# Self attention's rows are divided by their sums after the values are weighed, squares move to GpSimd, and two pieces of weighing stand one step later

## The chip, the cores and the metric

The kernel runs on one core of one Trainium2 chip. The metric is device time in microseconds (us). TensorE, written PE in the profile, multiplies matrices; ScalarE (ACT) applies functions; VectorE (DVE) and GpSimd (POOL) do elementwise work; SyncE (SP) starts transfers. Each engine runs its own instructions in program order and waits for the others by semaphores.

## The reference, cut to what matters

The program is a whole block with memory attention and feed forward, then two more layers. What is changed is its first mixer, at 512 positions, in float32:

```
fox:   s = q k^T / 8 + c_t - c_s, causal;  p = softmax(s);  o = p v        (8 heads of 64)
chunk: s = q k^T / 8 + bias, chunk-causal; p = softmax(s);  o = p v        (8 heads of 64)
mix = concat(rms_norm(o_fox), rms_norm(o_chunk)) @ w_out
```

`softmax` subtracts the row's maximum, takes `exp` and divides by the row's sum. `rms_norm` needs the sum of the squares of all heads' outputs. The memory, 256 positions of 1024, is normalised in the same stretch of time.

## The kernel before, in words

Every float32 operand of a product is held as a high part in a rounded type and a low part, the remainder; a product is three matmuls, high by high, high by low and low by high (`three`, L942 to L944). The high part is a copy by ScalarE, the low part a subtraction by VectorE or GpSimd.

Self attention is a pipeline of 64 steps. A unit is two heads and eight steps: step s has head 2(s//8) + s%2 and query block (s%8)//2, with 128, 256, 384 or 512 keys. I call a step by j = s%8 and its unit. Units 0 to 3 are the fox heads, 4 to 7 the chunk heads. In one step:

- TensorE `score_pair` makes scores for two heads at once in every second step, four steps ahead.
- VectorE takes the row's maximum (`maximum`, L2667).
- ScalarE takes the exponential, three steps ahead, and the row's sum with it (`exp`, L1915).
- VectorE inverts the sum (`invert`, L2673), and GpSimd multiplies the probabilities by it (`scale`, L854).
- TensorE turns the probabilities, a transpose per tile of 128 keys (`turn`, L1176). It waits for `scale`, and for the low part of two steps before, because there are two banks T.
- ScalarE writes the high part of the turned tile (`pt_high`, L1929), VectorE the low part (`pt_low`, L2680), into PT for even heads and PTH and PTL for odd ones.
- TensorE weighs the values of the unit before (`weigh`), in four pieces a head, a piece for each block of 128 keys, with 512, 384, 256 and 128 queries. The table `WEIGHED_AT` says in which j each piece comes. The values' two parts (VS) stand for both heads side by side, so a head's product fills 128 rows of bank O, of which 64 are its own.
- ScalarE copies those 64 rows into Y (`out`, L1941), even head in step 6, odd head in step 7, and then makes the next unit's high values (`stage_v`, L1908); GpSimd makes the low values (`low_v`, L847).

`pt_high` of step 0 and of step 1 overwrites what pieces (0, 0) and (1, 0) of the unit before read, and waits for them. In these two steps `exp` goes ahead of `pt_high`, and `maximum` ahead of `pt_low`.

Beside this, ScalarE squares the memory in steps 28 to 35 and Y in steps 36 to 63, VectorE adds up the squares (`norm_add`, L2612), scales the memory and makes its low parts in steps 41 to 59 (`self_norms`). After self attention GpSimd makes the low parts of the weight panels of the next product, mem_k (L806, then L902), and TensorE multiplies eight chunks of it; the sums of squares come after chunks 0 and 1 (L1150).

Of the kernel before, what the change touches and what calls it, by code (L numbers as in the profile page):

```python
# [17 lines left out]
F32 = mybir.dt.float32  # L18
F32R = mybir.dt.float32r
# [25 lines left out]
WEIGHED_AT = [[(0, 0), (0, 1)], [(1, 0), (1, 1)], [], [(0, 2)], [(1, 2)], [(0, 3)], [(1, 3)], []]  # L45
# [202 lines left out]
def program(nc, xT, memT, panels, ada, c, vecs, cons, gates_w, bias, pos, outT):  # L248
    ctx = ExitStack()
    with ctx:  # L250
# [88 lines left out]
        SELC = place(152, "SELC", [104, HEADS * P], F32R)  # L339

# [255 lines left out]
        for name in ("self", "mem", "mla"):  # L596
            att[name] = {k: sem(f"{name}_{k}") for k in (
                "v_high", "v_split", "scores", "max", "exp", "recip", "probs", "turned",
                "pt_high", "pt_split", "pv") + (("out",) if name == "self" else ())}
# [29 lines left out]
        def unit_v(name, u):  # L629

            if name == "self":
                return staged_v(V[:, :, u // 4 * S + u % 4 * P:u // 4 * S + u % 4 * P + P], u % 2, P)
# [170 lines left out]
        def _(pool):  # L803
# [53 lines left out]
            def attention(name):  # L857
# [4 lines left out]
                for s in range(steps):  # L862
# [4 lines left out]
                    if name == "self":  # L867
                        if s >= 12 and s % 8 == 7 and s // 8 + 1 < 8:
                            low_v(name, s // 8 + 1)
                        continue  # L870
                    n = (s - 6) // 4
                    if s >= 6 and s % 4 == 2 and n + 2 < heads_of(name):
                        low_v(name, n + 2)

# [23 lines left out]
            attention("self")  # L898
# [40 lines left out]
        def _(pe):  # L939
# [212 lines left out]
            def attention(name, scores, turned_tiles, pv, values):  # L1152
# [87 lines left out]
            def causal_pv(name):  # L1240

                def pv(n, slot, kb):
                    high, low = weights_in(name, n)
                    return three(O[n % 2][:, kb * P:S], VS[:, slot, 0, kb * P:(kb + 1) * P],
                                 VS[:, slot, 1, kb * P:(kb + 1) * P], high[:, kb, kb * P:S], low[:, kb, kb * P:S],
# [418 lines left out]
        def _(act):  # L1664
# [198 lines left out]
            def norm_square(name, m, source, width):  # L1863

                if m >= 2 or name != "mem":
                    act.wait_ge(s_add, first_of(ADD, name) + max(m - 1, 0))
                act.activation(nsq[:, m % 2, 0:width], source, ACT.Square).then_inc(s_sq, 1)

# [9 lines left out]
            def self_norms(s):  # L1878

                if 28 <= s < 36:  # L1880
                    if s == 28:
                        act.wait_ge(s_mem, 32)
                    norm_square("mem", s - 28, memc(s - 28), MEM)
                if s in (36, 37, 39, 40):
                    m = (36, 37, 39, 40).index(s)
                    act.wait_ge(att["self"]["out"], 2 * m + 2)
                    norm_square("fox", m, Y[:, m, :], S)
# [1330 lines left out]
```

## Time and profile before

| what | us |
|---|---|
| three timed runs | 2093.04, 2094.74, 2095.23 |
| median | 2094.74 |
| span of the profiled execution, first to last instruction | 2090.6 |
| self attention, first score to last weighing, on TensorE | 161.2 to 268.95 |
| TensorE busy over the span | 2054.0 (98%) |

No time is given for the profiled execution beside its span; the median of the timed runs is 4.1 us above that span. The page divides the span in 40 slices; self attention is in the fourth to the sixth, where GpSimd is busy for four to eight tenths and TensorE for nine or more.

### The profile page before, as it was taken

What the parts mean: (1) busy time and instruction counts of PE and PEld (TensorE: products, weight loads), DVE (VectorE), ACT (ScalarE), POOL (GpSimd) and SP (SyncE); (2) the same over time, 40 slices, a digit from 0 to 9 for tenths busy, and PEclk for the clock granted to TensorE, in tenths of its full rate; (3) what the DMA queues carried; (4) which work ended last, traced back from release to release, by engine and by line L of the source; (5) the groups of instructions that cost most, each with busy time, mean ns of one, the idle gap of its engine ahead of it and who ended that gap; (6) DMA issues with size and microseconds to landing.
All of it is one profiled execution on the core that took longest, in us unless ns stands there. A gap on an engine that the chain in (4) does not pass through costs nothing.

```text
span 2090.6 us, 28050 instructions
## 1 busy us (share of the span) xinstructions
PE 2054.0 (98%) x9901; PEld 1688.7 (81%) x9901; DVE 1120.3 (54%) x1769; ACT 875.4 (42%) x1493; POOL 964.1 (46%) x489
## 2 busy tenths in 40 slices
PE   9999999999999999999999999999999999999997
PEld 7877787888888888787778888888777888888887
DVE  4525834335677776763385543434566635434345
ACT  5326864455222222534386322323476653232233
POOL 3437885453445545334235244444445752444443
PEclk9999999999999999999999999999999999999999
DMA  6530052214466664364323133332322031332332
GB/s 214 193 101 21 11 202 91 81 41 161 157 225 213 227 229 155 101 221 161 86 51 106 51 101 93 97 100 91 91 81 81 1 101 52 100 99 92 100 93 89
DMA packets 70325, 238.40 MB, mean 114 GB/s; under 512 B 7776, under 2 KB 11232, under 8 KB 70112
## 3 DMA queue, kind: packets, MB, share of 16 engines
q1 hardware_dynamic: 70240, 237.26, 35.4%
q8 instruction: 54, 0.88, 0.2%
q14 instruction: 31, 0.25, 0.0%
HBM read 231.20 MB, written 2.10 MB: 112 GB/s over the span
## 4 chain that ended last, share of the span: by engine, by line
PE 82%; DVE 6%; ACT 4%; POOL 4%; issue 3%; DMA 1%; DVEq 0%; SPq 0%; ACTq 0%; POOLq 0%
PE bank L942 25%; PE bank L944 25%; PE bank L943 25%; PE bank L1049 1%; PE bank L1176 1%; PE bank L1091 1%; POOL WL L806 1%; POOL sq L854 1%; PE bank L1064 1%; POOL t L854 1%; DVE bank L2508 1%; DVE acc L2394 1%; PE bank L1255 0%; POOL CW L879 0%; DVE x L2512 0%
## 5 line engine op out<-in xcount | busy, mean ns | idle before, releaser
L806 POOL TENSOR_TENSOR WL<-stage,WH 128x1024 fp32r<-128x1024 f32 x256 | 633.4, 2475 | 888.4 <-ACT WH L1675 883.1
L1675 ACT ACTIVATE WH<-stage 128x1024 fp32r<-128x1024 f32 x256 | 271.4, 1061 | 812.5 <-PE bank L944 799.9
L942 PE MATMUL bank<-H,WH 128*128 128x512 f32 (+1 forms) x1132 | 438.0, 387 | 2.6 <-DVE H L2418 2.1
L944 PE MATMUL bank<-H,WL 128*128 128x512 f32 (+1 forms) x1132 | 437.1, 386 | 0.0
L943 PE MATMUL bank<-H,WH 128*128 128x512 f32 (+1 forms) x1132 | 437.0, 386 | 0.0
L2757 DVE TENSOR_TENSOR Y<-bank,Y 128x512 f32<-128x512 f32 x328 | 215.6, 684 | 94.9 <-PE bank L944 94.2
L942 PE MATMUL bank<-HID,WH 128*128 128x512 f32 (+1 forms) x688 | 264.3, 384 | 0.1
L943 PE MATMUL bank<-HID,WH 128*128 128x512 f32 (+1 forms) x688 | 264.2, 384 | 0.0
L944 PE MATMUL bank<-HID,WL 128*128 128x512 f32 (+1 forms) x688 | 264.2, 384 | 0.0
L942 PEld LDWEIGHTS bank<-H,WH 128*128 128x128 f32 x1132 | 212.6, 188 | 47.9 <-issue 3.4
L944 PEld LDWEIGHTS bank<-H,WL 128*128 128x128 f32 x1132 | 212.6, 188 | 42.9
L943 PEld LDWEIGHTS bank<-H,WH 128*128 128x128 f32 x1132 | 212.6, 188 | 42.8 <-issue 0.2
L2743 DVE SCALAR_TENSOR_TENSOR t<-bank,t 128x512 f32<-128x512 f32 x64 | 44.2, 691 | 266.8 <-ACT t L1997 266.7
L2483 DVE SCALAR_TENSOR_TENSOR ahead<-ahead,cond 128x1024 f32<-128x1024 f32 x102 | 175.7, 1772 | 8.5 <-DMA ahead<-ada 8.5
L2747 DVE TENSOR_TENSOR HID<-t,HID 128x512 fp32r<-128x512 f32 x86 | 121.2, 1409 | 65.9 <-ACT HID L2002 65.9
L942 PEld LDWEIGHTS bank<-HID,WH 128*128 128x128 f32 x688 | 129.3, 188 | 25.9 <-POOL WL L806 0.3
L944 PEld LDWEIGHTS bank<-HID,WL 128*128 128x128 f32 x688 | 129.3, 188 | 25.6
L943 PEld LDWEIGHTS bank<-HID,WH 128*128 128x128 f32 x688 | 129.3, 188 | 25.5
L2002 ACT ACTIVATE HID<-t 128x512 fp32r<-128x512 f32 x86 | 54.2, 630 | 57.3 <-DVE t L2743 51.6
L2657 DVE SCALAR_TENSOR_TENSOR QKL<-bank,QKH 128x512 fp32r<-128x512 f32 x40 | 27.3, 689 | 94.6 <-ACT QKH L1748 90.9
L854 POOL TENSOR_SCALAR sq<-sq,stat 128x256 f32<-128x256 f32 (+2 forms) x56 | 71.4, 1283 | 12.0 <-DVE stat L2673 11.6
L1049 PE MATMUL bank<-onesr,identr 128*128 128x512 f32 x271 | 72.5, 414 | 1.2 <-DVE onesr L2838 1.2
(468 smaller groups left out, 3612.2 us busy)
## 6 DMA issues: line engine op xcount, KB each, us to landing
stage<-panels SPq DMA_DIRECT2D x296, 512.0 KB, 3.6
ahead<-ada SPq DMA_DIRECT2D x102, 512.0 KB, 5.3
RAW<-panels SPq DMA_DIRECT2D x18, 512.0 KB, 4.0
apiece<-ada SPq DMA_DIRECT2D x10, 512.0 KB, 5.3
x<-xT SPq DMA_DIRECT2D x3, 1024.0 KB, 7.4
CS<-QKH SPq DMA_DIRECT2D x18, 128.0 KB, 2.4
outT<-x SPq DMA_DIRECT2D x16, 128.0 KB, 1.7
CS<-QKL SPq DMA_DIRECT2D x12, 128.0 KB, 2.4
```

The source lines that it names most:

```text
L806: pool.tensor_tensor(low_of(p, slot), stage[:, slot, :], high_of(p, slot).bitcast(F32), ALU.subtract).then_inc(s_split, 1)
L854: pool.tensor_scalar(prob[b][:, 0:w], prob[b][:, 0:w], stat[:, 8 + b:9 + b], None, ALU.mult)\
L942: pe.matmul(out, wh, rh, start=start, stop=False)
L943: pe.matmul(out, wh, rl, start=False, stop=False)
L944: return pe.matmul(out, wl, rh, start=False, stop=stop)
L1049: pe.matmul(out[:, :], identr[:, :], onesr[:, :].rearrange("p (a b) -> p a b", a=1).to_broadcast([P, 4, P]), start=True, stop=True)
L1675: act.activation(high_of(p, slot), stage[:, slot, :], ACT.Copy).then_inc(s_hisplit, 1)
L2002: act.activation(HID[:, slot, j, 0, :], t[:, j, :], ACT.Copy).then_inc(sm["high"], 1)
L2483: dve.scalar_tensor_tensor(source, source, 1.0, cond[:], ALU.mult, ALU.mult, accum_out=adac[:, column])\
L2743: ins = dve.scalar_tensor_tensor(t[:, j, :], up_banks[j][:, :], 0.0, t[:, j, :], ALU.max, ALU.mult)
L2747: dve.tensor_tensor(HID[:, slot, j, 1, :], t[:, j, :], HID[:, slot, j, 0, :].bitcast(F32), ALU.subtract).then_inc(sm["split"], 1)
L2757: dve.tensor_tensor(Y[:, m, :], (T + O)[m % 4][:, :], Y[:, m, :], ALU.add)\
```

## The change

1. **Division after weighing.** A new tile VO holds, for each of two units, for both parts and four key blocks, three columns of 64: the even head's values, a constant, the odd head's values. The constant is 1.0 in the high part and 0.0 in the low part. An even head is multiplied with the first two thirds, an odd head with the last two, so the 64 rows of bank O that held the other head's values now hold the row sums, 64 times over. `invert` and `scale` go; `turn` waits for `exp`. ScalarE takes the logarithm of the sums (`total_log`) and the exponential of its negative (`inverse`) into `rstd`; VectorE multiplies the head's 64 rows by it into Y (`out`). Each row of PT now carries weights that are not yet divided.
2. **Squares on GpSimd.** All sixteen squares of memory and Y go from ScalarE to GpSimd, each chunk of Y after `out`.
3. **Order.** `WEIGHED_AT` moves pieces (0, 0) and (0, 1) from j = 0 to 1 and (1, 0) and (1, 1) from 1 to 2. The bank O of head n is free for head n + 2 only after `out(n)`.
4. Four more memsets on VectorE at the start, and a smaller scratch area for transfers.

Core of the diff:

```diff
-WEIGHED_AT = [[(0, 0), (0, 1)], [(1, 0), (1, 1)], [], [(0, 2)], [(1, 2)], [(0, 3)], [(1, 3)], []]
+WEIGHED_AT = [[], [(0, 0), (0, 1)], [(1, 0), (1, 1)], [(0, 2)], [(1, 2)], [(0, 3)], [(1, 3)], []]
# gpsimd
-            attention("self")
+            self_attention()
             split_lows(PANEL0["mem_k"], RING0)
+            def self_attention():
+                outs = att["self"]["out"]
+                low_v("self", 0)
+                low_v("self", 1)
+                for s in range(64):
+                    if s >= 12 and s % 8 == 7 and s // 8 + 1 < 8:
+                        low_v("self", s // 8 + 1)
+                    if 28 <= s < 36:
...
+                        norm_square("mem", s - 28, memc(s - 28), MEM)
...
+                        pool.wait_ge(outs, 2 * m + 10)
+                        norm_square("chunk", m, Y[:, 4 + m, :], S)
+                pool.wait_ge(outs, 16)
+                norm_square("chunk", 3, Y[:, 7, :], S)
# tensor
-                    pe.wait_ge(sm["probs"], s + 1)
+                    pe.wait_ge(sm["exp" if name == "self" else "probs"], s + 1)
# scalar
+                def total_log(n):
                     act.wait_ge(sm["pv"], weighed(name, n, 3))
-                        act.activation(Y[half_rows[n % 2], n // 2, :], O[n % 2][half_rows[n % 2], :], ACT.Copy)\
-                            .then_inc(sm["out"], 1)
+                    if n >= 2:
+                        act.wait_ge(sm["out"], n - 1)
+                    act.activation(rstd[half_rows[n % 2], :], O[n % 2][half_rows[1 - n % 2], :], ACT.Ln)\
+                        .then_inc(sm["total_log"], 1)
+                def inverse(n):
+                    act.wait_ge(sm["total_log"], n + 1)
+                    act.activation(rstd[half_rows[n % 2], :], rstd[half_rows[n % 2], :], ACT.Exp, scale=-1.0)\
+                        .then_inc(sm["inverse"], 1)
+                    if name == "self" and s >= 12 and s % 8 == 7:
+                        inverse(2 * (s // 8 - 1))
                     if s + 3 < steps:
                         exp(s + 3)
+                    if name == "self" and s >= 16 and s % 8 == 0:
+                        inverse(2 * (s // 8 - 2) + 1)
                     if late:
                         pt_high(s)
-                    out(heads - 2)
-                    out(heads - 1)
+                    inverse(heads - 3)
+                    total_log(heads - 2)
+                    inverse(heads - 2)
+                    total_log(heads - 1)
+                    inverse(heads - 1)
# vector
+                def out(n):
+                    rows = half_rows[n % 2]
+                    dve.wait_ge(sm["inverse"], n + 1)
+                    dve.tensor_tensor(Y[rows, n // 2, :], O[n % 2][rows, :], rstd[rows, :], ALU.mult).then_inc(sm["out"], 1)
-                    if s + 3 < steps:
+                    if s + 3 < steps and name != "self":
                         invert(s + 3)
+                    if name == "self" and s >= 16 and s % 8 == 0:
+                        out(2 * (s // 8 - 2) + 1)
                     if late:
                         pt_low(s)
+                    if name == "self" and s >= 12 and s % 8 == 7:
+                        out(2 * (s // 8 - 1))
+                if name == "self":
+                    for n in range(heads_of(name) - 3, heads_of(name)):
+                        out(n)
+                    norm_add("chunk", 2, acc_chunk, S)
```

On ScalarE, from the end of a unit into the next one, before (Y gets the outputs, VS the high values, PT and PTH the high weights, t and sq the exponentials):

```order
L1941 ACTIVATE Y<-bank 64x512 [waits self_pv]
L1929 ACTIVATE PTH<-bank 128x4x128 [waits self_pv,self_turned]
L1915 ACTIVATE sq,stat<-bank,stat 128x256 [waits self_max,self_turned]
L1941 ACTIVATE Y<-bank 64x512 [waits self_pv]
L1908 ACTIVATE VS<-V 128x512 [waits self_pv]
L1915 ACTIVATE sq,stat<-bank,stat 128x256 [waits self_max,self_turned]
L1929 ACTIVATE PT<-bank 128x128 [waits self_pv,self_turned]
```

and now, at the same place:

```order
L1958 ACTIVATE rstd<-bank 64x512 [waits self_out,self_pv]
L1945 ACTIVATE PTH<-bank 128x4x128 [waits self_pv,self_turned]
L1963 ACTIVATE rstd<-rstd 64x512 [waits self_total_log]
L1928 ACTIVATE sq<-bank,stat 128x256 [waits self_max,self_turned]
L1958 ACTIVATE rstd<-bank 64x512 [waits self_out,self_pv]
L1920 ACTIVATE VO<-V 128x4x2x64 [waits self_pv]
L1928 ACTIVATE sq<-bank,stat 128x256 [waits self_max,self_turned]
L1963 ACTIVATE rstd<-rstd 64x512 [waits self_total_log]
L1945 ACTIVATE PT<-bank 128x128 [waits self_pv,self_turned]
```

Each copy has become a logarithm, and two exponentials of `rstd` stand between the turned tile of j = 7 and the high weights of the next unit's j = 0.

On VectorE at that place, now (`rstd` is the inverse sum, bank4 and bank5 are the two banks O):

```order
L2707 TENSOR_TENSOR PTL<-bank3,PTH 128x4x128 [waits self_pt_high]
L2694 TENSOR_REDUCE stat<-bank7 128x1 [waits self_scores]
L2720 TENSOR_TENSOR Y<-bank4,rstd 64x512 [waits self_inverse]
L2694 TENSOR_REDUCE stat<-bank0 128x1 [waits self_scores]
L2720 TENSOR_TENSOR Y<-bank5,rstd 64x512 [waits self_inverse]
L2707 TENSOR_TENSOR PT<-bank2,PT 128x128 [waits self_pt_high]
```

The odd head's product stands ahead of the low weights of j = 0, for which TensorE's turn of j = 2 waits.

On GpSimd, from self attention's end into the panels of mem_k, before (t and sq are the probabilities, WL the low panels):

```order
L854 TENSOR_SCALAR sq<-sq,stat 128x256 [waits self_recip]
L854 TENSOR_SCALAR t<-t,stat 128x384 [waits self_recip] x2
L854 TENSOR_SCALAR sq<-sq,stat 128x512 [waits self_recip] x2
L815 UNCONDITIONAL_BRANCH
L806 TENSOR_TENSOR WL<-stage,WH 128x1024 [waits panel_high] x2
```

and now (nsq are the squares, VO the low values):

```order
L849 TENSOR_TENSOR VO<-V,VO 128x4x2x64 [waits self_v_high]
L877 TENSOR_TENSOR nsq<-Y 128x512 [waits squares_added,self_out]
L849 TENSOR_TENSOR VO<-V,VO 128x4x2x64 [waits self_v_high]
L877 TENSOR_TENSOR nsq<-Y 128x512 [waits squares_added,self_out] x3
L817 UNCONDITIONAL_BRANCH
L808 TENSOR_TENSOR WL<-stage,WH 128x1024 [waits panel_high] x2
```

The first low panel stood behind the last `scale`; now it stands behind the square of the last two heads' outputs.

## Rows read from the trace of the kernel before

**Rows 1.** The page: busy time, share of the span and instructions.
```profile
PE 2054.0 (98%) x9901; PEld 1688.7 (81%) x9901; DVE 1120.3 (54%) x1769; ACT 875.4 (42%) x1493; POOL 964.1 (46%) x489
```

**Rows 2.** Stretches between turns of j = 7: length, busy of each engine, granted clock, DMA.
```profile
175.35:187.33 11.98, 11.28 (x87) 9.11 (x86) 8.23 (x25) 8.05 (x27) 8.88 (x9) 1.00 0.01 1
187.33:199.14 11.81, 11.23 (x87) 9.06 (x86) 7.81 (x25) 9.20 (x28) 9.82 (x10) 1.00 0.01 2
199.14:211.07 11.93, 11.46 (x86) 9.29 (x86) 7.47 (x25) 9.05 (x28) 9.55 (x10) 1.00 0.28 89
211.07:225.01 13.94, 12.43 (x88) 9.79 (x88) 11.42 (x33) 12.79 (x39) 11.39 (x10) 1.00 0.01 2
225.01:238.99 13.98, 11.87 (x87) 9.40 (x86) 11.29 (x32) 11.88 (x34) 10.58 (x9) 1.00 0.00 0
238.99:251.51 12.52, 11.86 (x87) 9.39 (x86) 10.64 (x34) 11.26 (x33) 10.83 (x10) 1.00 0.01 2
251.51:263.69 12.18, 10.70 (x67) 8.30 (x66) 8.71 (x26) 10.42 (x27) 10.49 (x10) 0.93 0.37 126
263.69:268.95 5.26, 5.26 (x30) 4.68 (x29) 3.52 (x3) 3.59 (x7) 5.26 (x3) 0.83 0.28 111
```

**Rows 3.** Waits of TensorE from 175 to 269 us, in total, times, longest.
```profile
PE bank L1176 <- POOL sq L854: 3.2, 6, 0.7
PE bank L1176 <- DVE PT L2680: 2.1, 2, 1.7
PE bank L1176 <- POOL t L854: 1.2, 4, 0.4
PE bank L1145 <- ACT t L1915: 0.9, 1, 0.9
```

**Rows 4.** Order of time on TensorE, unit of the second stretch: start, duration.
```profile
187.33 0.62 PE L1176 MATMUL bank<-con,sq 128*128 128x128 f32 x4
...
190.47 0.47 PE L942 MATMUL bank<-PTH,VS 128*128 128x512 f32 x1
...
191.78 0.38 PE L1176 MATMUL bank<-con,sq 128*128 128x128 f32 x2
```

**Rows 5.** The same unit on ScalarE.
```profile
187.98 0.60 ACT L1929 ACTIVATE PTH<-bank 128x512 fp32r<-128x512 f32 x1 [0.41 <-PE bank L1176]
...
189.06 0.59 ACT L1941 ACTIVATE Y<-bank 64x512 f32<-64x512 f32 x1
...
190.80 0.27 ACT L1929 ACTIVATE PT<-bank 128x128 fp32r<-128x128 f32 x1
```

**Rows 6.** Groups by line and shape, 158 to 275 us: busy, mean ns, idle before.
```profile
L1915 ACT ACTIVATION_READ_ACCUMULATOR sq<-bank,stat 128x1 f32 x32 | 6.3, 196 | 0.0
L847 POOL TENSOR_TENSOR VS<-V,VS 128x512 fp32r<-128x512 f32 x8 | 10.5, 1314 | 0.0
L2680 DVE TENSOR_TENSOR PT<-bank,PT 128x512 fp32r<-128x512 f32 x8 | 5.5, 691 | 5.5 <-ACT PT L1929 5.4
L2630 DVE SCALAR_TENSOR_TENSOR HML<-V,vec,HMH 128x256 fp32r<-128x256 f32 x8 | 4.0, 497 | 0.0
L806 POOL TENSOR_TENSOR WL<-stage,WH 128x1024 fp32r<-128x1024 f32 x2 | 4.7, 2388 | 0.0
L1685 ACT ACTIVATE WX<-RAW 128x1024 fp32r<-128x1024 f32 x2 | 2.1, 1050 | 0.4 <-DMA RAW<-panels 0.4
```

**Rows 7.** ScalarE behind self attention: a logarithm and an exponential.
```profile
272.94 0.69 ACT L1873 ACTIVATE logs<-bank,eps 128x512 f32<-128x512 f32 x1 [0.48 <-PE bank L1150]
273.66 0.60 ACT L1876 ACTIVATE bank<-logs 128x512 f32<-128x512 f32 x1
```

**Rows 8.** GpSimd's low panels, and TensorE's first chunk of mem_k.
```profile
263.60 4.74 POOL L806 TENSOR_TENSOR WL<-stage,WH 128x1024 fp32r<-128x1024 f32 x2
...
268.95 0.33 PE L942 MATMUL bank<-HMH,WH 128*128 128x256 f32 x1
```

**Rows 9.** Four microseconds at the lower clock, columns as in rows 2.
```profile
262.00:266.00 4.00, 3.85 (x15) 3.32 (x16) 1.49 (x3) 3.27 (x5) 4.00 (x4) 0.57 0.79 322
```

More of the change, by code:

```diff
@@ L597, in program @@
             att[name] = {k: sem(f"{name}_{k}") for k in (
-                "v_high", "v_split", "scores", "max", "exp", "recip", "probs", "turned",
-                "pt_high", "pt_split", "pv") + (("out",) if name == "self" else ())}
+                "v_high", "v_split", "scores", "max", "exp", "turned", "pt_high", "pt_split", "pv")
+                + (("total_log", "inverse", "out") if name == "self" else ("recip", "probs"))}
         s_pad = sem("queries_padded")
@@ L1243, in pv @@
                     high, low = weights_in(name, n)
-                    return three(O[n % 2][:, kb * P:S], VS[:, slot, 0, kb * P:(kb + 1) * P],
-                                 VS[:, slot, 1, kb * P:(kb + 1) * P], high[:, kb, kb * P:S], low[:, kb, kb * P:S],
+                    if name == "self":
+                        held = [VO[:, slot, hl, kb, n % 2:n % 2 + 2, :].rearrange("p h d -> p (h d)") for hl in range(2)]
+                    else:
+                        held = [VS[:, slot, hl, kb * P:(kb + 1) * P] for hl in range(2)]
+                    return three(O[n % 2][:, kb * P:S], held[0], held[1], high[:, kb, kb * P:S], low[:, kb, kb * P:S],
                                  kb == 0, kb == NT - 1)
@@ L1891, in self_norms @@
                     high_chunk("mem", s // 2 - 21, memc, lambda m: HMH[:, m, :], lambda m: col("zero"))
-                if s in (47, 55, 63):
-                    m = (s - 47) // 8
-                    act.wait_ge(att["self"]["out"], 2 * m + 10)
-                    norm_square("chunk", m, Y[:, 4 + m, :], S)
                 if s in (61, 63):
@@ L2118, in _ @@
             attention("self", self_norms)
-            act.wait_ge(att["self"]["out"], 16)
-            norm_square("chunk", 3, Y[:, 7, :], S)
             ring_panel(RING0 + 2)
@@ L2631, in self_norms @@
                                              ALU.add, ALU.subtract).then_inc(s_h, 1)
[L2632 to L2633 removed]
+                if s == 56:
+                    norm_add("chunk", 1, acc_chunk, S)
             def head_scaled(name, m):
@@ L2688, in out_low @@
                         .then_inc(s_h, 1)
-                maximum(0)
-                maximum(1)
-                invert(0)
-                maximum(2)
-                invert(1)
-                maximum(3)
-                invert(2)
+                def out(n):
+                    rows = half_rows[n % 2]
+                    dve.wait_ge(sm["inverse"], n + 1)
+                    dve.tensor_tensor(Y[rows, n // 2, :], O[n % 2][rows, :], rstd[rows, :], ALU.mult).then_inc(sm["out"], 1)
+                for s in range(4):
+                    maximum(s)
+                    if s and name != "self":
+                        invert(s - 1)
                 for s in range(steps):
@@ L2838, in _ @@
             dve.memset(onesr[:].bitcast(F32), 0.0).then_inc(s_eps, 1)
+            for slot in range(2):
+                dve.memset(VO[:, slot, 0, :, 1, :].bitcast(F32), 1.0)
+                dve.memset(VO[:, slot, 1, :, 1, :].bitcast(F32), 0.0)
             add_squares("x")
```

45 lines of the change are left out of this document (22 added, 23 removed).

## The prediction

> **What bounds the kernel now.** I read the page first: TensorE is busy for 98% of the span [rows 1], so nearly every stretch is worth only what it lets TensorE do sooner. Then I cut self attention at the turns of j = 7, one cut a unit [rows 2]; these eight stretches are where the change acts. The units take 11.8 to 14.0 us, and in each TensorE is idle for 0.5 to 2.1 us. The waits of that stretch [rows 3] say on whom: GpSimd's `scale` 4.4 us, VectorE's low weights 2.1 us, ScalarE 0.9 us, 7.4 us in all. That is the most that a perfect self attention can give back. Last I followed one unit on TensorE and ScalarE in order of time [rows 4, 5], because the new instructions stand between two of its events. The reader is to see there that the turn of j = 7 starts at 187.33, its high weights at 187.98, the high weights of j = 0 at 190.80, and the turn of j = 2 at 191.78. I count from T, the start of a unit's turn of j = 7.
>
> **What goes.** 64 `scale`, 64 `invert` and 64 reads of the accumulator (0.20 us each on ScalarE [rows 6]) go, and the 4.4 us that TensorE waits for `scale`. Squares leave ScalarE. What is late next is ScalarE.
>
> **The junction of two units.** Between the turned tile of j = 7 and the high weights of j = 0 ScalarE now has two inverses more. Before, the high weights of j = 0 started 2.82 us after those of j = 7 (190.80 less 187.98 [rows 5]). A copy of 0.59 us [rows 5] becomes a logarithm, 0.69 from the nearest row [rows 7]; two exponentials of 64 by 512 are put at 0.60 each, the row of 128 by 512, which I take for 64 rows too because the copy of 64 rows took 0.59 and one of 128 rows 0.60 [rows 5, 7]; two accumulator reads of 0.20 go. Sum 2.82 + 0.10 + 1.20 - 0.40 = 3.7. So the odd head's inverse ends at T + 0.65 + 3.7 = T + 4.35. Behind it VectorE has `out` of the odd head, 0.69 (a subtraction from a bank of 128 by 512 [rows 6]), and only then the low weights of j = 0, 0.28 by width from the same group. TensorE's turn of j = 2 waits for those: T + 5.35. Before it came at T + 4.45 (191.78 less 187.33 [rows 4]), and nothing held it. Bounds of the two exponentials: below 0.27 each, the narrowest high weights [rows 5], above 1.05, a copy of twice the width [rows 6]; per unit that is -0.7 to +0.9 us about my value.
>
> **What the order adds.** Weighing (1, 0) and (1, 1) took 1.31 us (190.47 to 191.78 [rows 4]) ahead of the turn of j = 2; it now comes after it, so it no longer fills the wait but lengthens what follows. Pieces (0, 0) and (0, 1) are ahead and run inside the wait. The turn of j = 3 then needs the low weights of j = 1, whose high weights wait for piece (1, 0): 0.17 of matmul end, 0.27 and 0.28 for the two parts, some 0.8 us with handing over, against 0.53 of piece (1, 1). That adds 0.26. From the turn of j = 2 to the next T it was 199.14 - 191.78 = 7.36 [rows 2, 4], of which 0.7 was the wait for `scale` ahead of the turn of j = 6, the longest of rows 3. Now 6.66 + 1.31 + 0.26 = 8.2. A fox unit becomes 5.35 + 8.2 = 13.55 instead of 11.81. A chunk unit keeps TensorE busy 0.63 longer (11.86 against 11.23 [rows 2]); its score pairs have two short matmuls more, but a busy time includes ends that lie in waits, so I take 0.25: 13.8 us.
>
> **Unit by unit, against rows 2.** Unit ending at 187.33: no output yet, so no logarithm, inverse or `out`; the `scale` wait of 0.7 goes, the two short waits come: -0.4. Next two: 13.55 and 13.65 for 11.81 and 11.93: +1.7 each. The fourth: GpSimd's square 3 of the memory stands behind its low values, which stand behind ScalarE's `stage_v`; VectorE's `norm_add` of step 31 waits for that square, ahead of `out` and the low weights of j = 0. From `stage_v`'s end at T + 3.4: 1.31, then a square of 256 columns 0.7, an addition 0.5, a maximum 0.5, `out` 0.69 and low weights 0.28, so T + 7.3 instead of T + 5.35. With 0.7 for the memory's sum on TensorE: 13.8 + 1.95 + 0.7 = 16.5 for 13.94, +2.5. The fifth: `norm_root` on ScalarE ahead of the junction 0.6, VectorE's memory work (0.5 each, every step [rows 6]) 0.45 in front of the turn of j = 6: 14.9 for 13.98, +0.9. The sixth: 14.3 for 12.52, +1.8. The seventh has no more scores after j = 3, 1.9 us less: 12.4 for 12.18, +0.2. Sum of the stage: +8.4 us.
>
> **The end.** The last stretch took 5.26 us from the turn of step 63 to the first chunk of mem_k [rows 2], which started without a wait, because GpSimd's low panel was long ready (263.60 plus 2.37, half of 4.74 [rows 8]). Now, from T: high weights until 2.1 (a panel copy of 1.05 in step 61 [rows 6] makes them late), inverse of head 12 to 2.6, logarithm of 13 to 3.3, panel copy to 4.35, inverse of 13 to 4.95, `out` of 13 to 5.6. Only then is bank O free for head 15's pieces; they and the rest, 2.6 us, end at 8.2. Then one after the other: logarithm and inverse of 14 and 15 until 10.7, `out` 11.4, square on GpSimd 1.31 (the subtraction of values of the same size [rows 6]) 12.7, low panel 2.37, TensorE 15.1. The extra is 9.9 us, 6.9 of them with TensorE wholly idle. Nothing covers it: mem_k's chunk 0 needs the panel, and every later product follows. Later panels take GpSimd 2.4 us against 2.9 us of a chunk, so they keep up and nothing is lost or regained.
>
> **The clock.** From 262 to 266 the granted clock was 0.57, after a stretch with three waits, and the level was 1.2 GHz for three of these microseconds. That cost 4.00 times 0.43 = 1.7 us [rows 9]. After 6.9 idle us I expect the same again on chunk 0: +1.7. The Trainium skill, "TensorE: Matmul & The Clock Gate", section "What's actually happening", says that an idle TensorE falls to half rate and comes back only after sustained work. The trace agrees for the short waits of rows 9 and says nothing of 6.9 us, since there is no such idle time in it.
>
> **Sum.** +8.4 + 9.9 + 1.7 = +20.0. The profiled span of 2090.6 becomes 2110.6, and the 4.1 us by which the median stands above the span are kept: 2114.8 us. The four memsets at the start are free: VectorE is idle before the first squares of x arrive.
>
> **Rivals.**
> - *The clock falls in the junctions too.* TensorE is idle for some 2.3 of the 3.5 us ahead of the turn of j = 2. The unit of 225 us had 1.7 us of wait in one piece [rows 3] and kept its clock [rows 2], the end did not [rows 9]. If five units pay 1.7 us each: +28.5, 2123 us.
> - *The junction is hidden.* If ScalarE reaches the inverses earlier than I think, the stage gives back its 7.4 us of waits in part or whole, and only the end costs. Whole: -7.4 + 9.9 + 1.7 = +4.2, 2099 us; half way between this and mine, 2107. For it: ScalarE is busy for only 9.1 of 11.9 us in a fox unit. Against: all but the first of the new instructions stand behind the turned tile of j = 7.
> - *The other side: end and stage both short.* TensorE runs without waits (-7.4), head 13's bank is free in time, and behind the last weighing only logarithm, inverse, `out`, square and panel of head 15 follow, 0.69 + 0.60 + 0.69 + 1.31 + 2.37 = 5.7, at full clock: -1.7, 2093 us. It decides where the turn of j = 2 comes by T + 3.2; I work out T + 5.35.
>
> **Chances.** My forecast 57%, the clock 20%, the hidden junction 17%, the other side 6%. The range of mine alone is 2109 to 2121 by the bounds of the exponentials (six units by -0.7 to +0.9); with the neighbours I give 2102 to 2127. A difference under 0.2%, 4.2 us, can't be told from none. The hidden junction in whole is at that border, so: faster 3%, same 4%, slower 93%.
>
> **What would show it.** Cut at the turns of j = 7, units 2 and 3 take 13.5 us, and the turn of j = 2 comes 5.3 us after T with a wait that names VectorE's low weights, behind `out`, behind a ScalarE inverse. GpSimd is nearly idle. The fourth unit is the longest. Between the last weighing and mem_k TensorE is idle for some 7 us, waiting for GpSimd's WL, and starts at the lower clock. I am wrong if the stage's TensorE waits shrink below 7.4 us in sum, or if GpSimd's WL is ready before the last weighing.

## The result, and the profile after

The changed kernel takes 2128.09 us (median of 4 runs, 2126.43 to 2130.78) against 2093.89 us for the kernel before on the same chip: 1.0165 times as long, 95% interval 1.0151 to 1.018, or 34.2 us more. The profiled spans are 2124.9 and 2090.6 us, 34.3 apart. The forecast was +20.0, with an upper end of 2127: slower, as predicted, but by much more, and 1.1 us outside the range.

The page of the changed kernel, busy time against [rows 1]: TensorE is busy for 10 us more, with the same number of matmuls, and idle for 24 us more.

```profile
PE 2064.3 (97%) x9901; PEld 1693.6 (80%) x9901; DVE 1127.3 (53%) x1725; ACT 874.4 (41%) x1429; POOL 903.9 (43%) x441
```

The stretches between the turns of j = 7, as in [rows 2]: length, busy time of each engine, granted clock.

```profile
176.21:188.47 12.26, 11.62 (x86) 8.98 (x86) 7.43 (x17) 7.20 (x18) 0.00 (x0) 1.00 0.01 1
188.47:204.80 16.33, 14.47 (x86) 10.98 (x86) 8.38 (x19) 9.95 (x22) 1.29 (x1) 0.79 0.00 1
204.80:218.89 14.09, 11.93 (x87) 9.23 (x86) 8.59 (x20) 10.13 (x22) 2.85 (x4) 1.00 0.24 76
218.89:238.72 19.83, 15.07 (x88) 11.30 (x88) 11.55 (x27) 10.04 (x22) 6.58 (x9) 0.83 0.00 1
238.72:257.95 19.23, 14.23 (x87) 10.68 (x86) 10.92 (x25) 11.01 (x26) 3.33 (x3) 0.82 0.01 1
257.95:272.76 14.81, 12.42 (x86) 9.42 (x86) 11.85 (x27) 11.36 (x26) 2.33 (x2) 1.00 0.00 0
272.76:286.19 13.43, 10.32 (x66) 7.69 (x66) 10.42 (x21) 10.07 (x21) 2.33 (x2) 1.00 0.33 119
286.19:302.27 16.08, 6.10 (x28) 5.09 (x28) 6.98 (x8) 8.17 (x13) 4.42 (x4) 0.81 0.27 94
```

They sum to 126.06 us against 93.60 before: 32.5 of the 34.3 us. Two things are to be seen. All stretches are longer, the fourth, the fifth and the last by most. And four of the eight have a mean clock of 0.79 to 0.83; before, only the last two were below 1.00. In this trace the clock falls five times: ahead of the turn of j = 2 in the second, fourth and fifth stretches, ahead of the last weighings (for 3.4 us, as it did once near the end of self attention before [rows 9]), and while TensorE waits for mem_k's low panel. A mean of 0.79 over 16.33 us is 16.33 x 0.21 / 0.5 = 6.9 us at 1.2 GHz.

TensorE's waits from 150 to 310 us: for what, total, times, longest. The waits for `scale` of [rows 3] are gone, and three others have come.

```profile
PE bank L1203 <- DVE PT L2707: 11.6, 8, 3.8
PE bank L969 <- POOL WL L808: 7.2, 1, 7.2
PE bank L969 <- DVE Y L2720: 6.5, 7, 2.8
PE bank L1203 <- DVE PTL L2707: 2.1, 7, 0.4
```

**A junction.** TensorE in the unit that starts at T = 188.47, in order of time, against [rows 4]: the turn of j = 7, piece (0, 0), the turn of j = 2. In brackets stands the wait.

```profile
188.47 0.63 PE L1203 MATMUL bank<-con,sq 128*128 128x128 f32 x4
...
191.53 0.47 PE L969 MATMUL bank<-PT,VO 128*128 128x512 f32 x1 [0.62 <-DVE Y L2720]
...
194.09 0.66 PE L1203 MATMUL bank<-con,sq 128*128 128x128 f32 x2 [1.11 <-DVE PT L2707]
```

ScalarE there, against [rows 5]:

```profile
189.14 0.60 ACT L1945 ACTIVATE PTH<-bank 128x512 fp32r<-128x512 f32 x1 [0.22 <-PE bank L1203]
189.63 0.62 ACT L1963 ACTIVATE rstd<-rstd 64x512 f32<-64x512 f32 x1
...
190.63 0.59 ACT L1958 ACTIVATE rstd<-bank 64x512 f32<-64x512 f32 x1
191.25 0.63 ACT L1920 ACTIVATE VO<-V 128x512 fp32r<-128x512 f32 x1
...
192.26 0.63 ACT L1963 ACTIVATE rstd<-rstd 64x512 f32<-64x512 f32 x1
192.92 0.28 ACT L1945 ACTIVATE PT<-bank 128x128 fp32r<-128x128 f32 x1
```

VectorE there:

```profile
192.93 0.69 DVE L2720 TENSOR_TENSOR Y<-bank,rstd 64x512 f32<-64x512 f32 x1 [1.08 <-ACT rstd L1963]
193.65 0.29 DVE L2707 TENSOR_TENSOR PT<-bank,PT 128x128 fp32r<-128x128 f32 x1
```

This is the predicted chain, link by link: ScalarE's second inverse ends at T + 4.4, `out` of the odd head and the low weights of j = 0 follow, and the turn of j = 2 comes at T + 5.62 (predicted 5.35) with a wait that names PT.

**The fifth stretch.** VectorE ahead of the turn of j = 2 at 247.35 (T + 8.63):

```profile
244.87 0.69 DVE L2639 TENSOR_TENSOR acc<-acc,nsq 128x512 f32<-128x512 f32 x1 [2.90 <-POOL nsq L877]
...
246.19 0.69 DVE L2720 TENSOR_TENSOR Y<-bank,rstd 64x512 f32<-64x512 f32 x1
```

and GpSimd:

```profile
242.55 1.29 POOL L849 TENSOR_TENSOR VO<-V,VO 128x512 fp32r<-128x512 f32 x1 [5.43 <-ACT VO L1920]
243.79 1.04 POOL L877 TENSOR_TENSOR nsq<-Y 128x512 f32<-128x512 f32 x1
```

The square of a fox chunk stands behind the unit's low values, VectorE's `norm_add` behind the square, and `out` behind that. It is the jam that was worked out for the fourth unit; here it had not been seen.

**The end.** The last weighing ends at 295.06. ScalarE behind it, one after the other with VectorE (the logarithm of head 14 and the inverse of 15 are shown), then GpSimd, and TensorE's first chunk of mem_k, in three views:

```profile
294.76 0.59 ACT L1958 ACTIVATE rstd<-bank 64x512 f32<-64x512 f32 x1 [3.77 <-PE bank L971]
...
296.66 0.63 ACT L1963 ACTIVATE rstd<-rstd 64x512 f32<-64x512 f32 x1
```

```profile
298.88 1.04 POOL L877 TENSOR_TENSOR nsq<-Y 128x512 f32<-128x512 f32 x1 [6.05 <-DVE acc_chunk L2639]
299.88 5.11 POOL L808 TENSOR_TENSOR WL<-stage,WH 128x1024 fp32r<-128x1024 f32 x2
```

```profile
302.27 0.58 PE L969 MATMUL bank<-HMH,WH 128*128 128x256 f32 x1 [7.21 <-POOL WL L808]
```

TensorE starts on mem_k at T + 16.1 instead of the predicted T + 15.1, and takes 0.58 us for a matmul that took 0.33 before [rows 8]: the lower clock.

### The profile page after: what moved, and what is told of

Same layout as the page of the kernel before. It is cut to its first block, busy times and chain, and to the rows that moved or that the text cites. A ratio compares the mean times of both kernels' runs of the same rounds, so it can differ in the third digit from the quotient of the medians.

```text
span 2124.9 us, 27908 instructions
## 1 busy us (share of the span) xinstructions
PE 2064.3 (97%) x9901; PEld 1693.6 (80%) x9901; DVE 1127.3 (53%) x1725; ACT 874.4 (41%) x1429; POOL 903.9 (43%) x441
## 4 chain that ended last, share of the span: by engine, by line
PE 65%; issue 16%; DVE 7%; POOL 6%; ACT 5%; DMA 1%; POOLq 0%; SPq 0%; DVEq 0%; ACTq 0%
PE bank L969 20%; PE bank L971 19%; PE bank L970 19%; POOL WL L808 4%; PE bank L1203 1%; PE bank L1076 1%; PE bank L1285 1%; PE bank L1091 1%; PE bank L1118 1%; DVE acc L2421 1%; DVE bank L2535 1%; DMA x<-xT 0%; DMA stage<-panels 0%; POOL CW L906 0%; DVE x L2539 0%
## 5 line engine op out<-in xcount | busy, mean ns | idle before, releaser
L2694 DVE TENSOR_REDUCE stat<-bank 128x1 f32<-128x128 f32 (+3 forms) x112 | 52.5, 473 | 26.7 <-PE bank L1291 24.2
```

Source lines behind the costliest of these rows:

```text
L2694: dve.tensor_reduce(stat[:, b:b + 1], score_bank(name, s)[:, 0:w], AX, ALU.max, negate=True)\
```

## The experiments

All were timed beside the kernel before, whose medians were 2092.7 to 2094.1. The ratios are estimated from the single executions, so they are near the ratio of the medians and not equal to it. The last column is when TensorE starts on mem_k, in the one profiled execution: roughly what the kernel has gained or lost up to the end of self attention. It is a scale of a few us only. The start of the first stretch alone, at 175.35 before, lies at 176.90 in e2, where nothing ahead of it was changed.

| kernel | median us | ratio to before, 95% | mem_k from |
|---|---|---|---|
| before | | 1 | 268.95 |
| changed | 2128.1 | 1.0165 [1.0151, 1.018] | 302.27 |
| e1_order_back | 2123.3 | 1.0136 [1.0118, 1.0154] | 296.15 |
| e2_order_alone | 2108.7 | 1.0078 [1.0061, 1.0095] | 284.12 |
| e3_panels_first2 | 2122.9 | 1.0134 [1.0117, 1.0151] | 295.46 |
| e4_squares_first | 2120.8 | 1.0132 [1.0115, 1.0149] | 295.12 |
| e5_odd_later | 2121.4 | 1.0129 [1.0112, 1.0146] | 294.72 |
| e6_clock_held | 2118.6 | 1.0125 [1.0108, 1.0142] | 295.01 |
| w1_all_moved | 2120.4 | 1.0118 [1.0102, 1.0135] | 295.75 |
| w2_early_outputs | 2100.8 | 1.0037 [1.0023, 1.0051] | 275.97 |
| w3_same_pieces_later | 2114.5 | 1.0106 [1.009, 1.0123] | 288.35 |
| w4_apart_on_gpsimd | 2099.5 | 1.0032 [1.002, 1.0044] | 274.50 |
| w5_panels_after_turns | 2097.4 | 1.0016 [1.0007, 1.0025] | 274.55 |

### The order against the rest: e1 and e2

e1 is the changed kernel with the table of before, e2 the kernel before with the new table.

```diff
-WEIGHED_AT = [[], [(0, 0), (0, 1)], [(1, 0), (1, 1)], [(0, 2)], [(1, 2)], [(0, 3)], [(1, 3)], []]
+WEIGHED_AT = [[(0, 0), (0, 1)], [(1, 0), (1, 1)], [], [(0, 2)], [(1, 2)], [(0, 3)], [(1, 3)], []]
```

> The changed kernel, but with the table of weighing pieces as before: (0,0) and (0,1) in j=0, (1,0) and (1,1) in j=1. Theory (the chain of ScalarE and VectorE at the junction, plus the clock): piece (0,0) now waits for the even head's output until T+3.0, (1,0) for the odd head's until T+5.0, and the turn of j=2 comes at T+6.4, but with 1.3 us less behind it, so a unit takes 13.0 us where it took 14.1 without a clock drop: six units save 3 to 6 us. The idle time is cut in two pieces, so fewer drops of the clock: 3 more. I expect 2118 to 2125 us. Rival (the new order is what costs, and division after weighing is cheap): near 2105 us. Rival (the outputs must come later, so the old order is worse): 2130 or more.

> The kernel before with only the new table of weighing pieces. Theory: the turn of j=2 comes some 0.3 us earlier after T, 1.6 us more stand behind it, and the wait for GpSimd's scale ahead of the turn of j=6 vanishes: a unit takes 12.3 us instead of 11.8, so 2097 us (+3). No drop of the clock in the junctions, the idle time there is under 1 us. Rival (the order alone carries a large part of the 34 us): 2105 us or more. Rival (the order costs nothing): 2094 us.

e1 came out at 2123.3, inside its expectation. TensorE now waits for the outputs, 18.5 us in 13 waits. Its waits in the unit from 199.96, for the even and the odd bank:

```profile
203.01 0.47 PE L969 MATMUL bank<-PT,VO 128*128 128x512 f32 x1 [1.05 <-DVE Y L2720]
205.25 0.47 PE L969 MATMUL bank<-PTH,VO 128*128 128x512 f32 x1 [0.69 <-DVE Y L2720]
```

e2 came out at 2108.7, where the rival had 2105 or more: the order alone costs 15.5 us, in a kernel without one new instruction. Two of its stretches between turns of j = 7, for the 11.81 and 13.98 of [rows 2]:

```profile
188.72:202.16 13.44, 11.78 (x87) 9.04 (x86) 7.68 (x25) 9.17 (x28) 9.81 (x10) 1.00 0.01 2
...
231.41:249.42 18.01, 14.96 (x86) 11.49 (x86) 11.33 (x32) 11.73 (x34) 10.30 (x9) 0.81 0.00 0
```

A unit takes 1.6 us more at full clock; the fifth waits 2.42 us at its turn of j = 2 and has a mean clock of 0.81, so the 15.5 us hold a fall of the clock too. The two parts alone cost 30.1 us (everything but the order) and 15.5 us (the order), in sum 45.6, the whole change 34.2: the second adds only 4 to 5 us to the first. Both make TensorE wait in the same junction, which would explain it; no run shows that this is the whole reason.

### The clock: e6

Dummy matmuls fill TensorE's long waits, and nothing else is changed: 4 to 15 ahead of each turn of j = 2, 10 ahead of the last weighings, 28 behind them.

```diff
+                    if name == "self" and s >= 10 and s % 8 == 2:
+                        for _ in range(FILL[s // 8]):
+                            pe.matmul(O[0][0:64, :], VO[:, 0, 1, 0, 1, :], ...)
+                    warm(G[1], 10)
+            warm(G[1], 28)
```

> The changed kernel with matmuls that change nothing (weights of zero added to a bank, or a bank nobody reads) placed where TensorE waits: 4 ahead of the turn of j=2 in each unit from the third on, 12 and 15 in the two units with the long waits, 10 ahead of the last weighing, 28 ahead of mem_k. They take about as long as the wait they stand in. Theory (part of the loss is the clock, which was at 1.2 GHz for 31 us in five stretches against 3.4 us before): the clock stays at 2.4 GHz in most of them, the second unit with outputs shrinks from 16.3 to 14.1 us, and the time falls by 8 to 12 us, to 2116 to 2120. Rival (the low clock lies beside waits anyway): within 2 us of 2128.

2118.6 us, 9.5 less than the changed kernel and inside the expectation. From 294 to 307 its mean clock is 1.00, where the changed kernel has 0.79 from 301 to 314. The second, fourth and fifth stretches keep full clock as well, with their turns of j = 2 as late as in the changed kernel (T + 5.62, T + 7.60, T + 8.62):

```profile
187.83:201.82 13.99, 12.74 (x91) 9.56 (x90) 8.39 (x19) 9.88 (x22) 1.30 (x1) 1.00 0.00 1
...
215.90:233.76 17.86, 15.69 (x100) 11.42 (x100) 11.57 (x26) 10.04 (x22) 6.62 (x9) 1.00 0.00 1
233.76:251.04 17.28, 15.74 (x101) 11.38 (x101) 10.93 (x25) 10.99 (x26) 3.33 (x3) 1.00 0.01 1
```

Against 16.33, 19.83 and 19.23 that is 2.3, 2.0 and 1.9 us for one fall in a unit. The whole 9.5 us is what the lower clock costs the changed kernel, possibly a little more, since the matmuls that fill a wait can also end a little late. Not all of it is new: the kernel before has one fall of its own, put at 1.7 us by [rows 9], so I estimate the clock's share of the 34.2 us at some 8.

### The end: e3

```diff
+                    if s == 63:
+                        split_lows(PANEL0["mem_k"], RING0)
                     if s in (47, 55, 63):
                         m = (s - 47) // 8
-                        pool.wait_ge(outs, 2 * m + 10)
+                        pool.wait_ge(outs, 16 if m == 2 else 2 * m + 10)
...
             self_attention()
-            split_lows(PANEL0["mem_k"], RING0)
```

Beside this the two last squares get a place of their own, `nsq_late`. In their old place they can't stay: mem_k's result is written there, so e3_panels_first, the same move without that place, has no time.

> The changed kernel (2128.1 us) with one thing moved: GpSimd makes the two low panels of mem_k as soon as its step 63 comes, ahead of squares 2 and 3 of the chunk heads, which are written to a free place (where PT stood) and wait for the last output. Theory (the end costs because GpSimd's panel stands behind square 3): mem_k's chunk 0 starts straight behind the last weighing, at T + 8.9 instead of T + 16.1, 7.2 us sooner, and with the 7.2 us of idle time goes the slow clock behind it, 1.7 to 3: 2118 to 2121 us. The sum of squares behind chunk 1 (T + 14.7) finds square 3 done at about T + 13.5. Rival (mem_k is held by something else too, a high panel or the sum of squares): less than 3 us gained, 2125 or more.

2122.9 us, between the two expectations. mem_k starts 6.8 us sooner and without a wait, as the theory has it, but at T + 10.0 instead of T + 8.9: the clock fell as the last weighings began and stayed low for six us. The whole gains only 5.2. Behind mem_k's first chunks TensorE waits for the sum of squares, and the clock falls once more:

```profile
304.54 1.57 PE L1180 MATMUL bank<-acc_chunk,con 128*128 128x512 f32 x2 [2.28 <-DVE acc_chunk L2643]
```

The square had been expected in time for it. Both late squares stand one behind the other there, and the addition behind the second one takes 2.75 us where the one before took 0.69. VectorE, then GpSimd:

```profile
299.74 0.69 DVE L2643 TENSOR_TENSOR acc_chunk<-acc_chunk,nsq_late 128x512 f32<-128x512 f32 x1 [1.16 <-POOL nsq_late L879]
301.73 2.75 DVE L2643 TENSOR_TENSOR acc_chunk<-acc_chunk,nsq_late 128x512 f32<-128x512 f32 x1 [1.29 <-POOL nsq_late L879]
```

```profile
301.58 5.13 POOL L932 TENSOR_TENSOR WX<-RAW,WX 128x1024 fp32r<-128x1024 f32 x2
```

These 2.06 us more are nearly all of TensorE's wait of 2.28; the addition runs beside the first half of a low panel, and w2 below shows the same thing. One stretch of e3 has a twin in the changed kernel: its second unit, alike in every instruction and every wait, kept full clock.

```profile
188.61:202.59 13.98, 11.79 (x86) 9.04 (x86) 8.38 (x19) 9.89 (x22) 1.29 (x1) 1.00 0.00 1
```

Against 16.33 of the changed kernel, that is 2.35 us for one fall of the clock, as in e6. It also shows that the same unit can lose its clock in one trace and keep it in the next. A gain of 5 to 7 us, as in e3, e4 and e5, can hold one such fall that came or did not come, so the traces' stretches are firmer ground than the totals.

### The jam of the squares: e4

```diff
-                    if s >= 12 and s % 8 == 7 and s // 8 + 1 < 8:
+                    if s in (15, 23, 47, 55):
                         low_v("self", s // 8 + 1)
...
                         norm_square("fox", m, Y[:, m, :], S)
+                    if s in (31, 39):
+                        low_v("self", s // 8 + 1)
```

> The changed kernel with one thing moved on GpSimd: in the units of steps 24 to 39 the low values stand behind the squares of their step and no longer ahead of them. Theory (in two units VectorE's out and low weights stand behind norm_add, which waits for a square that waits for low_v): the turn of j=2 comes at T + 5.6 in both, as in the others, instead of T + 7.6 and T + 8.6: -2.0 and -3.0 us, 2123 us; and if the long waits are what lowers the clock there, two stretches of 6.8 us at 1.2 GHz go too, another 3 to 6 us: 2117 to 2120. Rival (ScalarE, not GpSimd, is late there): under 1 us gained, 2127 to 2128.

2120.8 us, 7.3 less and just above the expectation. The turns of j = 2 come at T + 5.61 and T + 5.97 instead of 7.57 and 8.63, and the fifth stretch keeps full clock:

```profile
236.03:250.64 14.61, 12.30 (x87) 9.39 (x86) 10.85 (x25) 11.02 (x26) 2.66 (x3) 1.00 0.00 1
```

So of 19.23 us there 2.7 were the jam and 1.9 the clock that fell behind it. The fourth stretch still lost clock (mean 0.90).

### The odd head in the junction: e5

The inverse and `out` of the odd head stand behind the high and low weights of j = 0.

```diff
-                        inverse(2 * (s // 8 - 2) + 1)
                     if late:
                         pt_high(s)
+                        inverse(2 * (s // 8 - 2) + 1)
```

> The changed kernel with the inverse and the output of the odd head moved one place back, behind the high and the low weights of j=0, on ScalarE and VectorE. Theory (the turn of j=2 waits for these two instructions, 0.60 and 0.69): it comes at T + 4.3 to 4.6 instead of T + 5.6, and piece (1,0), behind that turn and a pair of scores, still finds its bank free: -1.0 to -1.3 us in each of six units, 2120 to 2122; less if the shorter waits keep the clock up, down to 2115. Rival (the wait only moves to piece (1,0), which needs the odd output): 2126 to 2128.

2121.4 us, inside the theory's range, but not quite by its sum. The turn of j = 2 comes at T + 4.82 (4.3 to 4.6 expected), with a wait of 0.3 instead of 1.1, and the third stretch takes 13.30 us for 14.09, 0.8 less (1.0 to 1.3 expected). The second stretch kept its clock here, 13.18 for 16.33, which is part of the gain. The turn of j = 2 in the third:

```profile
205.88 0.41 PE L1203 MATMUL bank<-con,sq 128*128 128x128 f32 x2 [0.32 <-DVE PT L2707]
```

### A version without the junction: w1 to w5

w1 has the moves of e3, e4 and e5, and the even head's inverse in j = 6, the next unit's values at j = 1, and (0, 0) and (0, 1) at j = 0.

> All three moves together, and three more: stage_v and low_v of the next unit at j=1 instead of j=7 (0.6 us out of the junction), the even head's inverse straight behind its logarithm in j=6, and the pieces (0,0) and (0,1) back at j=0 with (1,0) and (1,1) kept at j=2. Theory (the change loses by what stands between the turned tile of j=7 and the weights of j=0, and by the end): ScalarE has 1.25 + 0.5 + 0.69 + 0.5 us ahead of the high weights of j=0, they come at T + 3.2 and the turn of j=2 at T + 4.0 to 4.5, not held; the wait for scale is gone, fox units take 11.8 to 12.3 us and the whole 2093 to 2102 us. Rival (the division after weighing costs TensorE a wait for the bank O in any order): piece (0,0) waits some 1 us a unit and (1,0) too, 2105 to 2112.

2120.4 us: outside both expectations. TensorE waits for the even head's output at j = 0, which VectorE makes behind the low weights of j = 7, though its inverse had long been there:

```profile
207.53 0.47 PE L972 MATMUL bank<-PT,VO 128*128 128x512 f32 x1 [1.39 <-DVE Y L2723]
```

And the memory is loaded over the values of unit 3. Those were copied later, so the first square of the memory came 1.4 us behind the turn of j = 7 (in w2 1.1 us ahead of it), and the fourth stretch took 22.96 us. w2 mends both, and takes the odd head's logarithm and inverse straight behind the high weights of j = 7, with the old table:

```diff
 # scalar, j = 7, behind pt_high(s)
+                        total_log(2 * (s // 8 - 1) + 1)
+                        inverse(2 * (s // 8 - 1) + 1)
                     if s + 3 < steps:
                         exp(s + 3)
 # vector, j = 7
+                        out(2 * (s // 8 - 1))
                     if not late:
                         pt_low(s)
                     if s + 4 < steps:
                         maximum(s + 4)
+                        out(2 * (s // 8 - 1) + 1)
```

> In w1_all_moved TensorE waited 11.4 us for the outputs Y, because VectorE made the even head's output behind the low weights of j=7, and the memory came 3 us late because the values of unit 3 were copied later. Here: even head's logarithm and inverse in j=6 and its output ahead of the low weights of j=7; the odd head's logarithm and inverse straight behind the high weights of j=7, its output behind the maximum of j=7; stage_v at j=1 but in unit 2 at j=7; the old table of pieces; panels of mem_k ahead of the last squares, square 2 with its own place. Theory (the change loses only by where its new instructions stand): Y of the even head comes at T + 1.9, (0,0) starts there or 0.2 later, Y of the odd head at T + 3.5 for (1,0) at T + 3.1 to 3.6; scale's 0.7 is gone: fox units 11.5 to 12.0 us, last stretch 6.3, and without long waits the clock keeps: 2090 to 2096 us. Rival (each unit's bank O stays a tight loop and costs 0.5 to 1 us somewhere in each unit, and the clock falls at one or two places): 2098 to 2106.

2100.8 us: 27 of the 34 us are gone, but the total is in the rival's range and not in the theory's. Its second and third units take 11.69 and 11.79 us, the forecast of the theory and 0.1 below [rows 2], and no unit loses clock; it falls in the last stretch alone. What is left lies in the fourth stretch (15.68 us for 13.94), the seventh (14.29 for 12.18) and the last (8.68 for 5.26). The second stretch:

```profile
187.12:198.81 11.69, 11.34 (x87) 9.10 (x86) 8.64 (x19) 9.89 (x22) 1.29 (x1) 1.00 0.00 1
```

w3 is w2 with (1, 0) and (1, 1) at j = 2.

> The same kernel but with pieces (1,0) and (1,1) at j=2, (0,0) and (0,1) at j=0. Theory (TensorE's pieces are late by the order alone, as in e2_order_alone, which took 1.6 us a unit more than before with no new instruction): 1 to 1.5 us a unit slower than w2_early_outputs, 7 to 10 us in all. Rival (the bank of the odd head is free too late for j=1, so that the later place costs nothing): within 2 us of it or faster.

2114.5 us, 13.7 more than w2, more than either expectation. Its second and third units take 13.7 and 13.4 us at full clock, 2.0 and 1.6 more; the turn of j = 2 waits 1.3 to 2.0 us in each unit that the trace shows, with nothing left ahead of it to do, and the two pieces come on top. The rest is at least in part the clock, which in w3 falls from 226 to 236 and twice more.

In w2 four of the sixteen instructions by which VectorE scales the memory and makes its low parts lasted longer than their kind, 0.97, 1.37, 1.37 and 2.50 us; each reads two tiles in SBUF. Two of them, VectorE:

```profile
257.17 1.37 DVE L2656 SCALAR_TENSOR_TENSOR V<-V,vec,rstd_mem 128x256 f32<-128x256 f32 x1
...
261.96 2.50 DVE L2661 SCALAR_TENSOR_TENSOR HML<-V,vec,HMH 128x256 fp32r<-128x256 f32 x1
```

GpSimd at these times:

```profile
257.22 1.04 POOL L880 TENSOR_TENSOR nsq<-Y 128x512 f32<-128x512 f32 x1 [8.55 <-DVE Y L2724]
...
261.82 2.36 POOL L810 TENSOR_TENSOR WL<-stage,WH 128x1024 fp32r<-128x1024 f32 x1
```

The other twelve took 0.47 or 0.48. Each of the four ended 0.3 us behind a GpSimd instruction that also reads two tiles or squares one: low values, squares, a low panel. In the kernel before GpSimd was far busier, and still the group had a mean of 0.50 [rows 6]: there these instructions mostly met `scale`, which reads a tile and one column, and kept their 0.46 to 0.48 us in all fourteen cases, as here, VectorE and then GpSimd:

```profile
250.02 0.47 DVE L2625 SCALAR_TENSOR_TENSOR V<-V,vec,rstd_mem 128x256 f32<-128x256 f32 x1
```

```profile
249.44 1.56 POOL L854 TENSOR_SCALAR sq<-sq,stat 128x512 f32<-128x512 f32 x1
```

So the change replaced GpSimd work that does not hold VectorE by squares that do. In the changed kernel it shows too: an instruction of this kind beside a square took 1.16 us in the sixth unit and in the seventh. w4 moves them apart (panels behind the last HML, squares to steps 51 and 58), and the first ring panel to step 59:

```diff
+                        pool.wait_ge(s_h, before(MAKES, "mem") + KC)
                         split_lows(PANEL0["mem_k"], RING0)
-                if s in (61, 63):
+                if s in (59, 63):
```

> w2_early_outputs (2100.8 us, 8 above the kernel before) with its four remaining stalls moved apart. VectorE's instructions on SBUF alone lasted until a GpSimd instruction beside them ended (HML 2.50 instead of 0.47 us beside a low panel, V 1.37 instead of 0.47 beside a square): the low panels of mem_k now wait for the last HML and the last but two norm_add, the squares of chunk heads 0 to 3 stand at steps 51 and 58, the low values of unit 4 behind all squares of the memory, and the first ring panel in step 59 instead of 61. Theory (VectorE is held by GpSimd's instruction, and these holds are the waits of 0.7 us in each chunk unit, of 2.2 us at the turn of step 61 and part of the 2.2 us ahead of the last weighing): unit 4 -1.4, units 5 and 6 -0.7 each, unit 7 -2.5, the last stretch -0.9, in sum -6: 2093 to 2097 us, no difference from before. Rival (VectorE's long instructions are waits for something else and stay long): 2099 to 2101.

2099.5 us, in the rival's range. Its reason, though, is not the rival's: beside the panel nothing is held any more, but the squares at steps 51 and 58 met two other instructions of the kind (1.34 and 1.27 us), and the fifth and sixth units stay as they were (13.47 and 13.20 us for 13.48 and 13.24). The fourth unit is 2.0 shorter (13.71), and ScalarE stood still in step 59 for the panel's transfer:

```profile
262.03 1.06 ACT L1722 ACTIVATE WX<-RAW 128x1024 fp32r<-128x1024 f32 x1 [2.36 <-DMA RAW<-panels]
```

w5 has both ring panels in step 63, behind the last turned tile.

> w4_apart_on_gpsimd (2099.5 us) with both ring panels of ScalarE in step 63, behind the odd head's inverse. In w4 ScalarE waited 2.4 us in step 59 for the panel's transfer, so the turn of step 62 came 2.9 us late and 10.2 us at 1.2 GHz followed. Theory (that wait and the slow stretch are the rest of the loss): -2.9 for the wait, -0.9 for the high weights of step 62, and -3 to -5 for the slow stretch: 2091 to 2095 us, no difference from before. Rival (the second panel now holds the logarithm of head 14, and the end stays as late): 2097 to 2100.

2097.4 us, in the rival's range and not in the theory's. It is 0.16% above the kernel before, and the interval, 0.07 to 0.25%, excludes that there is no difference. It is the best of the changed versions, 30.7 us below the changed kernel, and does not beat the kernel before.

## Why the prediction was right and wrong

**Right.** The sign; that ScalarE is late in the junction and by which instructions (turn of j = 2 at T + 5.62 for 5.35; e5 takes 0.8 us a unit away); that the fourth unit jams (T + 7.57 for 7.3) and is the longest; that GpSimd's panel stands behind the last square and leaves TensorE idle for 7.2 us (6.9 predicted; e3). The sixth stretch was 14.81, predicted 14.3.

**The term of the clock, +1.7, was mis-sized.** This is the larger part of the error. The forecast let the clock fall once, behind the end. It fell in the second, fourth and fifth stretches too, for 2.3, 2.0 and 1.9 us by e6, 6.3 in sum, and e6 puts the whole at 9.5. The rival "the clock falls in the junctions too" named the mechanism and had 20%; it took five units at 1.7, where three paid about 2. The evidence against it was weighed wrongly: 1.7 us of idle time in one piece kept the clock [rows 2, 3], but the fall of the kernel before followed three short waits (0.3, 0.4 and 0.7 us from 259 to 262), and the second stretch of the changed kernel lost its clock with waits of 0.6 and 1.1 us, both within 3.2 us. The third, with the same waits, did not lose it. The price was low because the one fall of [rows 9] lasted 3.4 us; the falls in the three units lasted 6.8 us each. The Trainium skill, "TensorE: Matmul & The Clock Gate", section "HAM oscillation — how this bites in real kernels", tells of a kernel whose recurring waits for transfers lower the clock again in every round; this trace agrees for three of seven units, 6.8 us at the lower clock in each, with waits for other engines of 0.6 to 3.8 us.

**The step for the fifth unit, +0.9, left a wait out.** It named `norm_root` and the memory's work, but not that the fox square of step 39 stands behind `low_v` just as square 3 of the memory does in step 31. Measured: 19.23 us, 4.3 above the forecast of 14.9, 2.7 of it the jam by e4, and nearly all the rest clock.

**Smaller terms.** The third unit, at full clock, took 14.09 for 13.65, and the seventh 13.43 for 12.4, six times the increase that was forecast. At the end square 3 waited for the sum over chunk 2 as well (298.05 to 298.74), which with the rest made T + 16.1 of T + 15.1. The range of the forecast by its own bounds was also written as 2109 to 2121, where six units at -0.7 to +0.9 about 2114.8 give 2111 to 2120; it changes nothing in the outcome.

Sum of the errors: clock in three units 6.3; jam 2.7; the end 1.0; the first stretch, which starts 0.86 later, within what varies between these traces; 0.7 less than predicted behind the start of mem_k; and 4.1 over seven stretches, of which the fourth has 1.4 and the seventh 1.0. Together 14.3, as much as the span of 2124.9 lies above the 2110.6 of the forecast.

**What was never wrong but not seen.** Division after weighing need not cost anything in a fox unit: w2's second and third units are as short as before. 30.7 of the 34.2 us came from where the new instructions stand and from the order of the pieces, since w5 has the division and the squares on GpSimd and does without them.

**Open.** Why the second junction lost the clock and the third, alike, did not. Whether squares on GpSimd gain or cost by themselves: they hold VectorE up now and then, but the division with squares left on ScalarE was not tried. And the 3.7 us that w5 stands above the kernel before. In its trace the last stretch takes 9.03 us for 5.26, with a wait of 2.0 us ahead of the last weighings and the lower clock behind it, and the sixth unit 13.20 for 12.52; no run tests these two.

## What to carry to other kernels

When an edit puts instructions between two engines' events, list for every in-order engine what stands behind them, unit by unit; the jam that was found in one unit was missed in the next one. Where a forecast gives an almost full TensorE new waits, put a fall of the clock for each such place into the sum, by its chance (here three units of the six with the new waits paid 1.9 to 2.3 us each, and the same unit did in one trace and not in another), and do not leave it to a rival. Pieces of work that fill a wait lose their value when they are moved behind it: the late table cost 15.5 us with no other change. When work moves to GpSimd, look at what it does there: `scale` left VectorE alone, squares did not.

## What the runs showed of the hardware

- A VectorE instruction that reads two tiles in SBUF and meets a GpSimd instruction that reads two tiles, or squares one, mostly lasts until shortly behind the end of that one: 1.37 us beside a square and 2.50 beside a panel (w2), 0.47 alone. Beside `scale`, a GpSimd instruction on one tile and one column, it kept its 0.47 us in the kernel before. With one operand in PSUM it kept its length too (low weights of 128 by 256 beside w2's second panel: 0.41). The Trainium skill, "SBUF — State Buffer", section "Who interferes with whom", says that a VectorE instruction with two SBUF inputs contends with a GpSimd instruction that reads SBUF, and that one with at most one SBUF input does not, outside its 2-port modes. These traces agree with the second and, for squares, panels and low values, with the first. For `scale`, which reads SBUF as well, they show no hold on VectorE, and there the measurement decides.
- ScalarE on 64 rows of 512 took as long as on 128: copies 0.59 and 0.60 us, exponentials 0.63 and 0.60. The logarithm took 0.59 on 64 rows, and 0.69 on 128 rows with a column as bias [rows 7].
- A GpSimd square of 128 by 512 takes 1.04 us, and its subtraction of the same size 1.29.
